# A two-block transformer layer on one core: expert weights loaded in runs of four and three ring slots instead of two, two and three

## The reference, cut to what matters

```python
def _hier_moe(h, rg_w, rg_b, re_w, re_b, w1, w3, w2):
    ...
    def run(args):
        tok, e = args
        hb = hf[tok]
        return (jax.nn.silu(hb @ w1[e]) * (hb @ w3[e])) @ w2[e]

    y = lax.map(run, (slot_tok.reshape(n_blk, MOE_BLOCK), blk_exp)).reshape(P, D)
    out = jnp.zeros((T, D), h.dtype).at[slot_tok].add(y * slot_gate[:, None].astype(y.dtype))
    return out.reshape(B, S, D)
```

## Time and profile before

| | us |
|---|---|
| median of 3 runs (lowest to highest) | 911.45 (911.08 to 913.74) |
| the profiled execution's own time | 911.76 |
| its span in the trace | 910.0 |
| PE busy / DVE busy / ACT busy / POOL busy | 757.1 / 414.5 / 337.4 / 136.5 |
| mean granted TensorE clock, as a share of 2.4 GHz | 0.932 |
| bytes moved by DMA, mean rate | 299.01 MB, 329 GB/s |

### The profile page before, as it was taken

One profiled execution on the slowest core, in us unless ns is written; L12 is line 12 of the kernel. 1 busy time (PEld: TensorE's weight loads), 2 busy tenths in 40 slices (PEclk: granted clock), 3 DMA queues, 4 the chain that ended last, 5 costly groups with the idle time before them and its releaser, 6 DMA issues.

```text
span 910.0 us, 12726 instructions
## 1 busy us (share of the span) xinstructions
PE 757.1 (83%) x5292; PEld 524.8 (58%) x5292; DVE 414.5 (46%) x851; ACT 337.4 (37%) x664; POOL 136.5 (15%) x136
## 2 busy tenths in 40 slices
PE   9999999999999999999999984567574575665575
PEld 7986589999998877898786431123221222212223
DVE  5777777899998975899613110010100100001002
ACT  5766667666666667824723110001000000000012
POOL 0011043544431334103010000000000000000000
PEclk9999999999999999999999997789888888888888
DMA  9958964455553982646968999999999999999995
GB/s 352 423 209 315 427 243 162 185 186 185 186 185 108 387 340 79 266 175 236 341 256 328 431 444 424 427 433 431 432 428 431 435 432 429 431 442 418 433 423 242
DMA packets 19648, 299.01 MB, mean 329 GB/s; under 512 B 2176, under 2 KB 2560, under 8 KB 6144
## 3 DMA queue, kind: packets, MB, share of 16 engines
q1 hardware_dynamic: 19584, 298.13, 79.9%
HBM read 297.08 MB, written 1.05 MB: 328 GB/s over the span
## 4 chain that ended last, share of the span: by engine, by line
PE 51%; DMA 31%; DVE 12%; ACT 4%; issue 1%; POOL 0%; SPq 0%; DVEq 0%; POOLq 0%
PE ps L114 51%; DMA ring<-in_exps 31%; DVE ar L140 3%; DVE fr L132 2%; DVE sq L162 1%; DVE fr_h L132 1%; DVE yT L140 1%; ACT L120 1%; ACT yT L120 1%; PE ps L117 1%; DVE hT L140 0%; DVE ar L132 0%; ACT ar L123 0%; ACT sq L120 0%; ACT ar L120 0%
## 5 line engine op out<-in xcount | busy, mean ns | idle before, releaser
L114 PE MATMUL ps<-fr 128*128 128x256 f32 (+2 forms) x1332 | 213.3, 316 | 1.6 <-DVE fr L132 0.8
L114 PEld LDWEIGHTS ps<-fr 128*128 128x128 f32 (+1 forms) x1332 | 187.3, 189 | 21.0 <-DVE fr L132 2.7
L114 PE MATMUL ps<-ring,sq 128*32 128x512 f32 x936 | 127.6, 697 | 78.3 <-DMA ring<-in_exps 78.3
L114 PE MATMUL ps<-ring,ar 128*32 128x512 f32 (+4 forms) x784 | 87.8, 573 | 52.4 <-DMA ring<-in_exps 48.4
L114 PEld LDWEIGHTS ps<-ring,sq 128*32 128x32 f32 x936 | 31.4, 125 | 165.6 <-DMA ring<-in_exps 91.9
L132 DVE TENSOR_TENSOR ar<-ar,ps 128x512 f32<-128x512 f32 x9 | 6.2, 688 | 241.5 <-PE ps L114 240.2
L132 DVE TENSOR_TENSOR fr<-ring,fr 128x512 fp32r<-128x512 f32 (+2 forms) x119 | 92.5, 804 | 12.0 <-ACT fr L123 11.7
L123 ACT ACTIVATE fr<-ring 128x512 fp32r<-128x512 f32 (+2 forms) x143 | 84.7, 623 | 33.5 <-PE ps L114 30.4
L114 PEld LDWEIGHTS ps<-ring,ar 128*32 128x32 f32 (+1 forms) x784 | 26.3, 120 | 99.6 <-issue 45.6
L123 ACT ACTIVATE ar<-ps 128x512 f32<-128x512 f32 (+4 forms) x48 | 27.2, 570 | 151.8 <-PE ps L117 131.4
L132 DVE TENSOR_TENSOR ar<-ps,ar 128x512 f32<-128x512 f32 (+6 forms) x38 | 23.4, 632 | 120.7 <-PE ps L114 120.4
(11 more groups left out here) (193 smaller groups left out, 918.0 us busy)
## 6 DMA issues: line engine op xcount, KB each, us to landing
ring<-in_exps SPq DMA_DIRECT2D x21, 4096.0 KB, 28.5
ring<-in_exps SPq DMA_DIRECT2D x10, 6144.0 KB, 26.9
ring<-in_modw SPq DMA_DIRECT2D x12, 2048.0 KB, 8.9
ring<-in_exps SPq DMA_DIRECT2D x12, 2048.0 KB, 10.1
ring<-in_wup SPq DMA_DIRECT2D x11, 2048.0 KB, 12.3
ring<-in_wdown SPq DMA_DIRECT2D x5, 2048.0 KB, 7.9
ring<-in_win SPq DMA_DIRECT2D x4, 2048.0 KB, 11.8
ring<-in_exps SPq DMA_DIRECT2D x8, 1024.0 KB, 10.4
```

Source lines behind the costliest of these rows:

```text
L114: return Issue(self.e and self.e.matmul(o, l, r, start=start, stop=stop, skip_group_check=True))
```

## The change

The dictionary of runs changes, and nothing else. From slot 26 on the lengths are 4, 3, 4, 3 and so forth, up to 82 to 85 and 86 to 88, and one run of two (89 and 90) remains at the end.

```diff
--- before.py
+++ after.py
@@ -58,9 +58,9 @@
-RUNS = {19: 2}
-for _i in range(10):
-    RUNS.update({21 + 7 * _i: 2, 23 + 7 * _i: 3, 26 + 7 * _i: 2})
+RUNS = {19: 2, 21: 2, 23: 3, 89: 2}
+for _i in range(9):
+    RUNS.update({26 + 7 * _i: 4, 30 + 7 * _i: 3})
 RUN_OF = {j: next((a for a in RUNS if a <= j < a + RUNS[a]), j) for j in range(3 * NE)}
```

## The result

| | before | changed |
|---|---|---|
| median (lowest to highest) of 4 runs, us | 912.17 (911.08 to 913.74) | 926.45 (925.31 to 927.65) |
| ratio, 95% interval | 1 | 1.0155 (1.0141 to 1.0169) |
| profiled execution / its span, us | 911.76 / 910.0 | 925.31 / 923.5 |
| PE busy, us | 757.1 | 754.2 |
| mean granted clock | 0.932 | 0.917 |

The change makes the kernel 14.3 us slower, by the ratio 1.55%. The prediction was 921.5, or +10.1, with a range up to 926.0: the sign and the three places of the loss came out, the size did not, and the time lies just outside the range. Of the 5.0 us above the forecast, 0.7 are the base: the forecast stood on 911.45, the median of three runs, and a fourth run made it 912.17. Measured once more with the last experiments, the changed kernel took 925.17 against 912.03, that is +13.1 us.

The account below looks back on a forecast made before the run. From about 550 us the transfers bound the kernel, so only a dry queue costs time. +10.5 for the dry places and -0.4 for run boundaries gave +10.1 us, 921.5 against a median of 911.45; range 915.5 to 926.

Parts of the forecast that it names:

- The price of a dry load: Four slots loaded into a dry queue land after 8.6 + 3 x 4.85 = 23.2 us, about 2 us being start without bytes.
- place A: Slots 33 to 36, turn of 9.0 us after 35: queue dry, 40 to 43 land at 652.9, +6.2 us.
- Part (1): Nine issues of SP fall away, each 0.33 us, beside SP's waiting: worth nothing.
- (2): Nine fewer run boundaries: 0 to -0.9 us, taken as -0.4.
- The rival of 64 KB rows: Rows of 64 KB move slower; 5% slower would add 8.7 us, about 929; 5 in 100.
- a start of its own for each load: Rival: each load pays a start hidden in the rates; at 2 us a run, -8 us, 903; 2 in 100.
- The queue never runs dry: Rival: PE reaches slots 36 and 50 earlier, leaving only the run boundaries, 0 to -0.9 us, 911; 6 in 100.
- only place A counts: Rival: B comes a little earlier and catching-up engines absorb the rest: +5, 916.5; 10 in 100.
- B: Slots 47 to 50, turn after 47: queue dry again, 54 to 57 land at 725.4, adding 4.2 us.
- place C: Slots 54 to 57, inner turn after 55: a tie, total shift +10.2 to +12.1 us by slot 64, 10.5 taken.
- part (4): SP's wait for all four former slots: PE has 14.55 us less 2 us of start, 12.5 us, before the queue is dry.
- every run has 4 us to spare: Runs of four after place C: without a turn PE takes 8.5 of the 12.5 us, so no loss.

Follow-up runs that it names:

- harmless runs of four: Changed kernel with runs of four only at 26, 68, 75 and 82, the five at 33, 40, 47, 54, 61 as runs of two: 911.77 against 912.14.
- the experiment on the rows: Kernel before, its pairs of runs of two laid out in DRAM in rows of 64 KB, each DMA taking its 32 KB half: 912.64 against 913.16.
- the kernel without A: Changed kernel with 33 to 36 and 40 to 43 as runs of two again: 920.02 against 913.16, ratio 1.0075.
- the row moved: Changed kernel with the row that PE spreads moved from the turn of group 2 to that of group 4: 923.62 against 912.14.
- kernel with products: Changed kernel with products into an unused PSUM bank in PE's pauses before slots 33 (31), 47 (44) and 54 (60): 923.69 against 912.14.
- products with the right counts: Changed kernel with such products, but 53 before slot 47 and 76 before slot 54: 921.5 against 912.03, changed kernel 925.17.
- late landings: Kernel before, but readers of a pair of runs of two wait until both have landed; issues unchanged: 914.54 against 913.16, ratio 1.0015.
- the kernel with a warm end: Kernel before with products into an unused PSUM bank before slots 92 (4) and 93 (9): 911.9 against 912.03, ratio 0.9999.
- the late issue: Kernel before, but SP waits for all four slots' former contents before the first run of two of each pair: 918.21 against 913.16, ratio 1.0056.

## Why the prediction was right or wrong

**The bound: right.** The transfers set the end of this stage, and the loss is idle time of the DMA engines: 12.0 us missing in three stretches of the windows.

**The three places: right.** Nothing else ran dry, the order of the places and the two that were to be large came as forecast (7.2 and 4.2 us of idle transfer). The kernel with only harmless runs of four showed it by the other side.

**The price of a dry load: right as a whole, not in its parts.** 23.2 us forecast from one load of a single slot, 23.12, 22.78 and 23.16 measured. But "about 2 us" of it were put down as a start without bytes. At place A the load was issued at 631.68, and the windows around it are:

```profile
631.00:632.00 1.00, 1.00 (x16) 0.33 (x12) 0.00 (x0) 0.00 (x0) 0.00 (x0) 1.00 0.00 0
632.00:633.00 1.00, 1.00 (x12) 0.26 (x8) 0.00 (x0) 0.00 (x0) 0.00 (x0) 1.00 2.76 918
```

So the first packets start some 1 us after the issue. In the earlier trace rows the window that is left out, 479 to 480, has a share of 1.47 already.

**Part (1), (2) and the rows: right within what can be told.** 0 to -0.9 us were forecast for fewer run boundaries; the harmless four gave -0.4 us with an interval of 1 us to either side, for four of the nine runs, so nothing can be said beyond the bounds. The rival of 64 KB rows fell with the experiment on the rows and the harmless four, that of a start of its own for each load with the harmless four (it asked for 2 us each, 8 in all). The fit of the Trainium skill that stood beside that rival ("DMA: Bandwidth & Descriptors", section on the anatomy of one DMA) is given there for DMAs that GpSimd issues, and the loads here are issued by SP. "The queue never runs dry" fell with the empty windows, "only place A counts" with the 4.0 us of B and the +6.9 us of the kernel without A.

**The term of place A was too small: 6.2 forecast, 8.1 measured.** Two amounts make the 1.9 us. The step "PE does three slots, 6.7 us" took 7.57, since I took the price of three slots from pauses after which the clock was lower for a shorter time (granted clock 0.80 and 0.79 over the two stretches of the earlier trace rows, 0.68 here): 7.61 in the repetition and 7.66 with the row moved say that this is no chance of one execution. And slots 33 to 36 landed at 612.96 instead of 611.95, 1.0 us later. The start of slot 23 at 559.77, 558.48 before, shows that a lag of 1.3 us was there before the first run of four: it belongs to the execution. With products keeping PE warm, the 7.57 became 5.36.

**The term of place C failed in its mechanism: 0.1 forecast, 1.5 measured.** I had both values (+10.2 and +12.1 as sums), called it a tie and took a value "near the lower end, since the issue comes before the last landing". The load was issued at 739.54, 2.1 us ahead of the landing before it at 741.61, and it landed 23.16 us after its issue, 21.1 after that landing, where a load that queues needs 19.4. The wrong step is that of part (4), "less 2 us of start": not 2 us but the whole 3.8 that a dry load costs have to lie between the issue and the landing ahead. Five loads of four from the traces, in us:

| load | issued ahead of the landing before it | landed after its issue | landed after that landing |
|---|---|---|---|
| 61 to 64, kernel with products | 1.0 | 23.2 | 22.2 |
| 61 to 64, changed kernel | 2.1 | 23.2 | 21.1 |
| 61 to 64, row moved | 2.9 | 23.2 | 20.3 |
| 61 to 64, products with the right counts | 3.6 | 22.9 | 19.4 |
| 68 to 71, changed kernel | 4.8 | 24.2 | 19.4 |

The later of two times holds: 19.4 us after the landing before it, or 23.2 us after the issue. Of my two values for C it is always the larger that counts, 761.2; there was no tie. It is not exact: 68 to 71 with the row moved, issued 4.7 us ahead, landed 20.5 after the landing before it, its last engine having fallen 1.0 us further behind the first.

**The margin behind place C was too large.** I wrote that "every run has 4 us to spare". At 772.39 the load of 68 to 71 went out 4.8 us ahead of the landing at 777.2, and 3.8 were needed: 1 us was to spare. Four slots after the landing had taken 9.51 us, not 8.5.

**The end of the kernel was not free.** I wrote that the end "moves as it is". Slot 93 was there at 903.44, 12.3 us after the 891.1 of before; the last product of PE ended at 916.14 against 902.58, 13.6 us later. Of the 1.2 us between, 1.0 are products at the lower clock, 2.96 us at 903.48 where the kernel before took 1.93:

```profile
558.48 3.46 PE L114 MATMUL ps<-ring,ar 128*32 128x512 f32 x16 [10.90 <-DMA ring<-in_exps]
...
885.36 3.17 PE L114 MATMUL ps<-ring,ar 128*32 128x256 f32 x32 [1.14 <-DMA ring<-in_exps]
891.14 1.93 PE L114 MATMUL ps<-ring,ar 128*32 128x256 f32 x32 [2.62 <-DMA ring<-in_exps]
...
901.48 1.10 PE L114 MATMUL ps<-ar 128*128 128x64 f32 x8
```

(these rows are of the kernel before; the first is slot 23 of the account of place A). The repetition of the changed kernel has it too, 3.12 us, but so have the kernel before with the rows of 64 KB pitch (3.46) and with late landings (3.00), and in the profile above the slow piece is the one before, 3.17 us at 885.36. Whether the change brings this about or the execution is not shown; the kernel with a warm end does not settle it, since it was the kernel before.

**The sum.** For the profiled executions it closes: 8.1 + 4.0 + 1.5 = 13.6 us by slot 64, where 10.5 was forecast; the -0.4 for run boundaries does not show; 1.3 us come back by slot 93, and 1.2 are lost again at the end. That is 13.5, and 925.31 - 911.76 = 13.55. The 1.3 that came back are what the prediction called the catching-up of late engines: the last engine was 3.4 us behind the first at slot 64 and 4.6 at slot 93 in the kernel before, 1.8 and 1.8 in the changed one. That they and the 1.2 us of the end cancel is luck.

**The range** should have reached to the sum of the dry value of C and the slow slot that I had named for each place. That is 12.1 - 0.4 + 1.7 at one place, 924.9, and with a second slow slot 926.6, and the 926.45 would have been inside. All of its parts stood in the prediction, which gives no reason for ending the range at 926. I say this with the result in hand.

## What to carry to other kernels

A load that joins n slots of a ring lands late for the first and is issued late for the last. What it costs is not read from the load but from the other side: the consumer's whole time from its landing to the use of its last slot, at the clock it will have after a pause and with every turn that falls inside, against what is still queued behind it, less the whole extra price of a dry load (3.8 us here: 23.2 for four slots against 19.4 in a queue), not only its start. If that margin is negative, the stage loses the difference each time; if it is positive, nothing or little. And where a stage already moved its bytes at 431 GB/s with a DMA share of 1.00, as this one did, fewer and larger loads had nothing to win.

## What the runs showed of the hardware

- A load into a dry queue has a nearly fixed price. Four slots (8 MB) landed 21.7 to 23.2 us after their issue in all 20 dry cases of seven profiles, 16 of them at 22.8 or more; that is 19.4 us of bytes and 2.3 to 3.8 us besides. The spread between the 16 engines is in it: in the four cheaper cases (21.7 to 21.9 us) the last engine's increment came 0.5 to 0.6 us after the first one's, in the others 1.1 to 2.0 us. The Trainium skill ("DMA: Bandwidth & Descriptors", section on the anatomy of one DMA) fits about 2.0 us fixed, for DMAs that GpSimd issues; here, with loads issued by SP, it was more.
- "Dry" begins before the last landing. A load issued 1.0 to 3.6 us ahead of the landing before it landed 22.9 to 23.2 us after its issue, like one into an empty queue; one issued 4.8 us ahead landed 19.4 us after the landing before it, like any that queues.
- The granted clock after a pause isn't a constant price, and the length of the pause alone doesn't give it. Three slots took 5.36 us with PE kept busy; after waits for a landing of 2.4 to 11.5 us they took 5.36 to 8.3 us: 6.77 after 9.07 in the kernel before, 7.57 after 8.60 in the changed kernel, 8.02 after 4.11 with the row moved, 5.36 after 3.53 with the late issue. In the changed kernel the clock row for its 7.57 us is 0.68:

```profile
613.00:620.00 7.00, 7.00 (x48) 1.80 (x48) 0.00 (x0) 0.00 (x0) 0.00 (x0) 0.68 1.04 445
```

- In the kernel with products before slot 47, PE stood still for 2.6 us between the last of them and the landing, at a granted clock of 1.00; the clock was 0.61 in the 3 us after it, and the slot took 3.01 us, where 1.92 is its time at the full clock.
